# Sample states as the moving operand on four column groups, state increments on four row groups, in a fused hybrid decoder step

## What is computed

```python
def step(S, inp):                       # one chunk; the sample has one chunk of 4 tokens
    qg_c, kd_c, u_c, w_c, qk_c, gl_c = inp
    v_new = u_c - w_c @ S
    o = qg_c @ S + qk_c @ v_new
    S = S * gl_c + kd_c.T @ v_new
    return S, o
```

## Time and profile before

| | |
|---|---|
| median of 3 runs | 1909.12 us (1908.06 to 1911.35) |
| the profiled execution | 1911.12 us |
| its span, first to last instruction | 1909.3 us |
| mean granted TensorE clock | 0.995 |
| TensorE busy (PE) | 1800.0 us, 94% |
| VectorE busy (DVE) | 556.5 us, 29% |
| ScalarE busy (ACT) | 388.0 us, 20% |
| HBM read | 519.14 MB |

### The profile page before, as it was taken

One profiled execution on the slowest core, in us unless ns is written; L12 is line 12 of the kernel. 1 busy time (PEld: TensorE's weight loads), 2 busy tenths in 40 slices (PEclk: granted clock), 3 DMA queues, 4 the chain that ended last, 5 costly groups with the idle time before them and its releaser, 6 DMA issues.

```text
span 1909.3 us, 22816 instructions
## 1 busy us (share of the span) xinstructions
PE 1800.0 (94%) x8060; PEld 933.9 (49%) x8060; DVE 556.5 (29%) x1811; ACT 388.0 (20%) x922; POOL 19.5 (1%) x37
## 2 busy tenths in 40 slices
PE   7999999999998999999999999999999999999998
PEld 4777777777775433433333333333333333334333
DVE  2334434434434200321323213232132311224113
ACT  1424524524523111311000111001010010002103
POOL 0000000000000000000000000000000000000000
PEclk9999999999999999999999999999999999999999
DMA  8333433433404461599999999999999999999401
GB/s 253 100 95 102 126 94 103 124 94 104 124 28 149 152 250 73 199 419 428 427 428 427 427 427 427 427 427 427 428 426 427 425 427 425 424 424 384 168 22 50
DMA packets 208462, 519.92 MB, mean 272 GB/s; under 512 B 18664, under 2 KB 139488, under 8 KB 157152
## 3 DMA queue, kind: packets, MB, share of 16 engines
q1 hardware_dynamic: 198160, 513.83, 69.0%
q0 software_dynamic: 2304, 4.86, 0.7%
q10 hardware_dynamic: 7968, 0.83, 0.3%
HBM read 519.14 MB, written 12.26 MB: 278 GB/s over the span
## 4 chain that ended last, share of the span: by engine, by line
PE 79%; DMA 17%; DVE 2%; ACT 1%; issue 1%; SPq 0%; DVEq 0%; ACTq 0%
PE ps L582 75%; DMA ring<-in_w_down_dram 17%; PE ps L585 3%; DMA x<-in_x_sample_dram 0%; PE ps L1082 0%; ACT hb L1210 0%; ACT ring L1210 0%; SPq L477 0%; DMA pp_rows<-hb 0%; DVE ring L1694 0%; PE ps L710 0%; PE ps L730 0%; DVE ring L1745 0%; PE ps L731 0%; DVE x L2011 0%
## 5 line engine op out<-in xcount | busy, mean ns | idle before, releaser
L582 PE MATMUL ps<-ring,hT 128*64 128x512 f32 x2048 | 457.0, 596 | 25.6 <-DMA ring<-in_w_up_dram 25.6
L582 PE MATMUL ps<-hT,ring 128*128 128x288 f32 x1536 | 410.1, 414 | 0.0
L582 PE MATMUL ps<-ring,mixT 128*64 128x512 f32 (+2 forms) x1408 | 365.6, 598 | 35.9 <-DMA ring<-in_w_down_dram 25.6
L582 PEld LDWEIGHTS ps<-hT,ring 128*128 128x128 f32 x1536 | 283.3, 192 | 70.4 <-issue 0.5
L582 PEld LDWEIGHTS ps<-ring,hT 128*64 128x64 f32 x2048 | 145.7, 137 | 308.4 <-issue 305.8
L582 PEld LDWEIGHTS ps<-ring,mixT 128*64 128x64 f32 (+2 forms) x1408 | 124.8, 144 | 240.2 <-issue 238.3
L582 PE MATMUL ps<-ring,hb 128*128 128x512 f32 (+2 forms) x512 | 143.7, 512 | 0.0
L582 PE MATMUL ps<-mixT,wpT 128*128 128x512 f32 (+1 forms) x384 | 130.1, 601 | 0.0
L582 PEld LDWEIGHTS ps<-ring 128*128 128x128 f32 (+3 forms) x880 | 115.7, 186 | 29.0 <-DVE ring L1767 7.9
L582 PE MATMUL ps<-ring 128*128 128x128 f32 (+3 forms) x880 | 123.8, 272 | 1.7 <-DVE ring L1754 1.6
L1210 ACT ACTIVATE ring<-ps 128x256 f32<-128x256 f32 (+5 forms) x176 | 47.5, 310 | 294.4 <-PE ps L582 256.8
(11 more groups left out here) (248 smaller groups left out, 1096.7 us busy)
## 6 DMA issues: line engine op xcount, KB each, us to landing
ring<-in_w_gate_dram SPq DMA_DIRECT2D x128, 1024.0 KB, 22.5
ring<-in_w_up_dram SPq DMA_DIRECT2D x128, 1024.0 KB, 24.4
ring<-in_w_down_dram SPq DMA_DIRECT2D x128, 1024.0 KB, 22.0
ring<-in_w_in_dram SPq DMA_DIRECT2D x48, 1024.0 KB, 5.6
ring<-in_w_out_dram SPq DMA_DIRECT2D x16, 1024.0 KB, 11.0
ring<-in_w_ple_gate_dram SPq DMA_DIRECT2D x16, 1024.0 KB, 13.3
hb<-in_state_delta_dram SPq DMA_DIRECT2D x8, 512.0 KB, 5.2
out_dram<-hb SPq DMA_DIRECT2D x8, 512.0 KB, 3.7
```

Of the source, the lines that this page charges most:

```text
L582: return pe.matmul(out, lhsT, rhs, start=start, stop=stop)
```

## The change

For the sample, the roles in the products with the states are swapped and the small matmuls are placed on parts of the array:

- Step 3: the state becomes the moving operand (128 columns), the 32-column block of WQ the weights, each sequence on column group b % 4 of the array. The two halves (b < 4, b >= 4) accumulate in one bank; WQ is zero except for each sequence's own 8 columns. ScalarE copies the result out as SQs (`SQ_r`).
- Step 4: v is corrected by tokens: the matmul of XTs4 (four copies of XTs side by side) and vb, plus a matmul of a constant selecting matrix `pick_w` and SQs in the same bank. The transpose and VectorE's subtraction go. The result has the 32 tokens four times, on all 128 partitions.
- Step 5: the q.S part is added by one more matmul with `pick_q`. VectorE's addition and `os_r` go.
- Step 6: Vm is two masked copies on 128 partitions; four matmuls of 32 rows on 256 columns, each on its own row group and with its own bank (3 to 6). They wait for `os_p` too; the sum of squares goes to bank 7 and waits for `S2_r` too.
- The triangular solve's first level (L1763 to L1767) writes XTs in four copies, four operations of VectorE where there was one, before the one that lets TensorE go on (`lev_new`).
- Step 1 makes the sample's k on all four partition groups (4 matmuls for one transpose), step 2 loses the uT matmul, and the prologue's sample decays are made four times.

```diff
@@ constants
-              ("seq", row // SEQ_LEN == np.arange(SEQS)[None, :]),
+              ("seq", row % SAMPLE // SEQ_LEN == 2 * (row // SAMPLE) + np.arange(2)[None, :]),
+              ("pick_w", -1.0 * (row == solved_row(col % SAMPLE))), ("pick_q", (row == solved_row(col) + SEQ_LEN)[:, :SAMPLE]),
@@ tensor: prologue
-            mm(ps[0:SAMPLE, 3, 16:24], C("btriu", SAMPLE), g[0:SAMPLE, 2, :])
-            mm(ps[0:SAMPLE, 3, 40:48], C("ball", SAMPLE), g[0:SAMPLE, 2, :]).then_inc(dec["prep_mm"], 1)
+            for r in range(0, P, 32):
+                mm(ps[r:r + 32, 3, 16:24], C("btriu", SAMPLE), g[0:SAMPLE, 2, :])
+                last = mm(ps[r:r + 32, 3, 40:48], C("ball", SAMPLE), g[0:SAMPLE, 2, :])
+            last.then_inc(dec["prep_mm"], 1)
@@ tensor: head, step 1
-                    pe.transpose(ps[0:n, 5, t * P:(t + 1) * P], qk[:, 1, off:off + n], C("ident"))
+                    if t < 2:
+                        pe.transpose(ps[0:n, 5, t * P:(t + 1) * P], qk[:, 1, off:off + n], C("ident"))
+                    else:
+                        for r in range(0, P, 32):
+                            mm(ps[r:r + 32, 5, t * P:(t + 1) * P], qk[:, 1, PROMPT:TOK], C("ident"))
@@ step 2
-                mm(ps[:, 5, PROMPT:TOK], vb[0:SAMPLE, 2, :], XTs[0:SAMPLE, :])
@@ step 3
-                    last = mm(ps[:, 2, b * 8:(b + 1) * 8], Sold[:, b, :], WQ[:, b, :])
+                    g = 32 * (b % 4)
+                    last = mm(ps[g:g + 32, 2, 0:P], WQ[:, 32 * b:32 * b + 32], Sold[:, b, :], b < 4, b >= 4)
@@ step 4
-                pe.wait_ge(E["vnT_r"], h1)
-                pe.transpose(ps[0:SAMPLE, 5, 0:P], vnTs, C("ident")).then_inc(E["vnTT"], 1)
+                pe.wait_ge(E["SQ_r"], h1)
+                mm(ps[:, 5, 0:P], XTs4[0:SAMPLE, :, :], vb[0:SAMPLE, 2, :], True, False)
+                mm(ps[:, 5, 0:P], C("pick_w"), SQs, False, True).then_inc(E["vns_mm"], 1)
@@ step 5
-                mm(ps[:, 4, PROMPT:TOK], vns[0:SAMPLE, :], QKTs[0:SAMPLE, :]).then_inc(E["o_mm"], 1)
+                mm(ps[:, 4, PROMPT:TOK], vns[0:SAMPLE, :], QKTs[0:SAMPLE, :], True, False)
+                mm(ps[:, 4, PROMPT:TOK], SQs, C("pick_q"), False, True).then_inc(E["o_mm"], 1)
@@ step 6
-                for q in range(2):
-                    last = mm(ps[:, 5 + q, :], kd[0:SAMPLE, 2, :], Vm[0:SAMPLE, 4 * q:4 * q + 4, :])
+                pe.wait_ge(E["os_p"], h1)
+                for r in range(4):
+                    rows = slice(32 * r, 32 * r + 32)
+                    last = mm(ps[:, 3 + r, 0:2 * P], kd[rows, 2, :], Vm[rows, 0:2, :])
                 last.then_inc(E["dS_mm"], 1)
                 pe.wait_ge(E["osq_r"], h1)
-                mm(ps[:, 3, 0:TOK], C("ones"), osq).then_inc(E["oss_mm"], 1)
+                pe.wait_ge(E["S2_r"], h1)
+                mm(ps[:, 7, 0:TOK], C("ones"), osq).then_inc(E["oss_mm"], 1)
@@ scalar: head
-                f(uTs, ps[:, 5, PROMPT:TOK])
...
+                act.wait_ge(E["SQ_mm"], h1)
+                f(SQs, ps[:, 2, 0:P]).then_inc(E["SQ_r"], 1)
                 pieces_out()
-                act.wait_ge(E["vnTT"], h1)
-                f(vns[0:SAMPLE, :], ps[0:SAMPLE, 5, 0:P]).then_inc(E["vns_r"], 1)
+                act.wait_ge(E["vns_mm"], h1)
+                f(vns, ps[:, 5, 0:P]).then_inc(E["vns_r"], 1)
...
-                act.wait_ge(E["os_r"], h1)
+                act.wait_ge(E["os_p"], h1)
                 f(osq, oS, ACT.Square).then_inc(E["osq_r"], 1)
@@ vector: head, level 1
-                        tt(XTs[0:SAMPLE, :], XTs[0:SAMPLE, :], ps[0:SAMPLE, 7, 256:256 + SAMPLE], ALU.subtract)
+                        for r in range(3, -1, -1):
+                            tt(XTs4[0:SAMPLE, r, :], XTs[0:SAMPLE, :], ps[0:SAMPLE, 7, 256:256 + SAMPLE], ALU.subtract)
@@ vector: head, steps 3 to 6
-                v.wait_ge(E["SQ_mm"], h1)
-                SQ = ps[:, 2, 0:64].rearrange("p (b c) -> p b c", c=8)
-                sq4 = lambda a: a.rearrange("p (b c) -> p b c", c=SEQ_LEN)
-                tt(sq4(vnTs), sq4(uTs), SQ[:, :, 0:SEQ_LEN], ALU.subtract).then_inc(E["vnT_r"], 1)
...
-                for b in range(SEQS):
-                    last = ts(Vm[0:SAMPLE, b, :], vns[0:SAMPLE, :], C("seq", SAMPLE)[:, b:b + 1], None, ALU.mult)
+                for i in range(2):
+                    last = ts(Vm[:, i, :], vns, C("seq")[:, i:i + 1], None, ALU.mult)
                 last.then_inc(E["Vm_r"], 1)
-                v.wait_ge(E["os_p"], h1)
-                os4 = sq4(oS[:, PROMPT:TOK])
-                tt(os4, os4, SQ[:, :, SEQ_LEN:], ALU.add).then_inc(E["os_r"], 1)
+                v.wait_ge(E["o_mm"], h1)
                 v.wait_ge(E["s2_st"], snap(h * 16 + 1))
...
-                              in1=ps[:, 5 + b // 4, (b % 4) * P:(b % 4 + 1) * P], op0=ALU.mult, op1=ALU.add)
+                              in1=ps[:, 3 + b // 2, (b % 2) * P:(b % 2 + 1) * P], op0=ALU.mult, op1=ALU.add)
```

More of the change, by code:

```diff
@@ L57, in _constants, with solved_row @@
     same = (row // SEQ_LEN) == (col // SEQ_LEN)
+    def solved_row(token):
+        b = token // SEQ_LEN
+        return 32 * (b % 4) + 2 * SEQ_LEN * (b // 4) + token % SEQ_LEN
     parts = [("ident", row == col), ("triu", row <= col), ("before", row < col), ("ones", row >= 0 * col),
@@ L214, in trunk @@
         Xs = w(SAMPLE)
-        XTs = w(SAMPLE)
+        XTs4 = w(4, SAMPLE)
+        XTs = XTs4[:, 0, :]
         T1 = w(2, P)
@@ L219, in trunk @@
         wT = w(2, P)
-        uTs = w(SAMPLE)
-        WQ = w(SEQS, 2 * SEQ_LEN)
+        WQ = w(272)
+        WQ_cols = WQ.rearrange("p (h x) -> p h x", h=2)[:, :, 0:P].rearrange("p h (g c) -> p h g c", g=4)
+        SQs = w(P)
         S1 = w(P)
@@ L224, in trunk @@
         vn1 = w(P)
-        vnTs = w(SAMPLE)
         vns = w(P)
-        Vm = w(SEQS, P)
+        Vm = w(3, P)
         Sold = w(SEQS, P)
@@ L317, in trunk @@
                  "ln_sq", "vn_r", "mixA_mm", "mixA_r", "uw_mm", "uw_cp", "WQ_r", "S1_mm", "S1_r", "SQ_mm", "wS_mm",
-                 "vn1_r", "vnT_r", "vnTT", "Vm_r", "vns_r", "o_mm", "S2_r", "Sn_r", "os_p", "os_r", "osq_r", "oss_mm", "rn_r", "or_r",
+                 "vn1_r", "SQ_r", "vns_mm", "Vm_r", "vns_r", "o_mm", "S2_r", "Sn_r", "os_p", "osq_r", "oss_mm", "rn_r", "or_r",
                  "mixB_r")
@@ L901, in between @@
                         last.then_inc(R["lgT_mm"], 1)
-            pe.wait_ge(E["os_r"], HEADS)
+            pe.wait_ge(E["os_p"], HEADS)
             for k in range(KT - 1):
@@ L1328, in head @@
                     f(kbg[0:n, t, :], kt, scale=hs[0:n, t, 3:4])
-                    f(kd[0:n, t, :], kt, scale=hs[0:n, t, 4:5])
+                    f(kd[:, t, :], ps[:, 5, t * P:(t + 1) * P], scale=hs[:, t, 4:5])
                     last = f(vb[0:n, t, :], vt, scale=hs[0:n, t, 2:3])
@@ L1350, in head @@
                 f(us[:, :, :], ps[:, 5, 0:256].rearrange("p (t n) -> p t n", t=2))
-                f(uTs, ps[:, 5, PROMPT:TOK])
-                f(WQ[:, :, 0:SEQ_LEN], ps[:, 6, PROMPT:TOK].rearrange("p (b c) -> p b c", c=SEQ_LEN))
+                f(WQ_cols[:, :, :, 0:SEQ_LEN], ps[:, 6, PROMPT:TOK].rearrange("p (h g c) -> p h g c", h=2, c=SEQ_LEN))
                 f(wT[:, 1, :], ps[:, 6, P:2 * P]).then_inc(E["uw_cp"], 1)
@@ L1367, in head @@
                 act.wait_ge(E["oss_mm"], h1)
-                rstd([(orn, ps[:, 3, 0:TOK], P)], P, E["or_r"])
+                rstd([(orn, ps[:, 7, 0:TOK], P)], P, E["or_r"])
                 pieces_out()
@@ L1607, in _ @@
             v.memset(pre[:, :, :, :], 0.0).then_inc(M["wpt_T"], 1)
+            v.memset(WQ, 0.0)
             ch(v.memset(raw[:, :, 0:PAD], 0.0))
@@ L1648, in _ @@
             cp(pre[:, 5, 0:2, :], ps[:, 3, 0:16].rearrange("p (t c) -> p t c", t=2))
-            cp(pre[0:SAMPLE, 5, 2, :], ps[0:SAMPLE, 3, 16:24])
+            cp(pre[:, 5, 2, :], ps[:, 3, 16:24])
             cp(pre[:, 6, 0:2, :], ps[:, 3, 24:40].rearrange("p (t c) -> p t c", t=2))
-            ch(cp(pre[0:SAMPLE, 6, 2, :], ps[0:SAMPLE, 3, 40:48]))
+            ch(cp(pre[:, 6, 2, :], ps[:, 3, 40:48]))
             ch.wait()
             tt(pre[:, 7, 0:2], pre[:, 6, 0:2], pre[:, 5, 0:2], ALU.subtract)
-            v.memset(pre[:, 7, 2], 0.0)
             ch(v.memset(zero[:, :], 0.0))
             ch.wait()
-            tt(pre[0:SAMPLE, 7, 2], pre[0:SAMPLE, 6, 2], pre[0:SAMPLE, 5, 2], ALU.subtract).then_inc(dec["prep_v"], 1)
+            tt(pre[:, 7, 2], pre[:, 6, 2], pre[:, 5, 2], ALU.subtract).then_inc(dec["prep_v"], 1)
             v.wait_ge(dec["prep_a"], 3)
@@ L1794, in head @@
                         tt(mixT[:, bass.ds(h, 1), :].rearrange("p a n -> p (a n)"), mA, uT, ALU.mult).then_inc(E["mixA_r"], 1)
-                cp(WQ[:, :, SEQ_LEN:], qg[:, PROMPT:TOK].rearrange("p (b c) -> p b c", c=SEQ_LEN)).then_inc(E["WQ_r"], 1)
-                v.wait_ge(E["SQ_mm"], h1)
-                SQ = ps[:, 2, 0:64].rearrange("p (b c) -> p b c", c=8)
-                sq4 = lambda a: a.rearrange("p (b c) -> p b c", c=SEQ_LEN)
```

(3 more changed lines are left out.)

## The result

| | before | after |
|---|---|---|
| median of 5 runs | 1909.12 us (1908.06 to 1911.35) | 1900.06 us (1898.35 to 1902.88) |
| the profiled execution | 1911.12 us | 1899.4 us |
| its span | 1909.3 us | 1897.6 us |
| the fourth head, from start to start | 71.69 us | 70.78 us |
| TensorE busy | 1800.0 us, 94% | 1790.4 us, 94% |

The ratio of after to before is 0.9954 (0.9942 to 0.9966). The forecast was 1900.2. A second pair of runs gave 1910.46 before and 1900.47 after, ratio 0.9947 (0.9933 to 0.996).

What follows compares the result with a forecast made beforehand. Heads bound by TensorE's own stream, experts by their transfers: -1.14 us a head, -9.1 in 8 heads, prologue about +0.2, sum -8.9, so 1909.1 to 1900.2 us; range 1898 to 1903, 8 in 10 1896.0 to 1905.0.

Steps and rivals of the forecast that it cites:

- a loss of 0.2: Prologue: 12 more passes from its four-fold small matmuls were to add about 0.2 us outside the heads.
- the added waits: TensorE's waits on `SQ_r`, `os_p`, `S2_r` and Vm: projection passes were to cover them, so priced at nothing.
- visit: TensorE's switch to part of the array and back: 0.10 us per shape change, about 0.22 in all among short passes.
- Rivals A: Increments on row groups: weights load in turn, 0.90 us a head; sum -5.1, median 1904.0 us; chance 0.12.
- B: Increments: row groups run in turn, 1.72 us a head as before; sum +1.4, median 1910.5 us; chance 0.07.
- C: Increments: row groups in turn, each load in the open, 2.5 us; sum +7.7, median 1916.8 us; chance 0.05.
- Rival D: Short column-group passes run in turn at 0.06 us each; sum -2.8, median 1906.3 us; chance 0.04.
- The solve's delay: Solve's first level: four VectorE copies instead of one make `lev_new` 0.29 us later, uncovered on TensorE; +0.29 a head.
- The experts: Stretch bound by its DMA transfers: moves forward with shorter heads, as long as before, neither eating nor adding gain.
- the clock's spells: Last head: the clock falls while TensorE waits; a spell more or less is worth up to 2 us.
- the 0.56: Increments on row groups, by the skill's 3.07 times: 0.56 us a head, making the sum -7.9.

Runs made afterwards that it cites:

- e6: Changed kernel with the XTs4 and vb matmul issued earlier, beside the other 32-row matmul, and `pick_w` adding to it there; 1894.8 us, ratio 0.9924.
- e1: Changed kernel with all four increment matmuls on rows 0 to 31, one row group in turn (wrong results); 1909.91 us, ratio 1.0002 to before.
- e2: Changed kernel with all eight state matmuls on column group 0, in turn (wrong results); 1909.77 us, ratio 1.0001 to before.
- e3: Changed kernel with XTs written once in the solve's first level and its other three copies made behind the second level; 1898.88 us, ratio 0.9942.
- e9: The kernel before, run and profiled again without an edit; 1909.74 us, ratio 1.0001 to its other runs.
- e7: Changed kernel with VectorE writing the sample's k four times and one 128-column transpose replacing four matmuls; 1896.0 us, ratio 0.9928.
- e10: The changed kernel, run and profiled again without an edit; 1900.47 us, ratio 0.9947 to before.

## Why the prediction was right, and where its sum was off

The median moved by 9.06 us, where the sum said 8.9. That it came out so close is luck. Two errors stand against each other: the heads gained 7.3 us (8 x 0.91) and not 9.1, and about 1.8 us came from outside their sum, where I had a loss of 0.2. A head of 70.78 us is also outside the 0.15 either way that I had allowed for 70.55. The mechanism was right: both kinds of groups run side by side, and the added waits are covered.

| step of the sum, us a head | predicted | measured |
|---|---|---|
| step 1, sample's k on four groups | +0.33 | +0.35 |
| solve, copies ahead of `lev_new` | +0.29 | +0.29 |
| step 2, uT gone | -0.22 | -0.22 |
| step 3, states on column groups | -1.03 | -1.02 |
| step 4, tokens and `pick_w` | +0.56 | +0.72 |
| step 5, `pick_q` | +0.22 | +0.24 |
| step 6, increments on row groups | -1.29 | -1.27 |
| the head | -1.14 | -0.91 |

- **Step 4 is the term that was mis-sized,** +0.72 for +0.56. I priced its visit as one "among short passes", 0.22. That price comes from 32-row matmuls with 32 moving columns: in before's records of them the first pass after the change of shape is followed by the next in 0.133 us (302.759 to 302.892). In step 4 the moving operand has 128 columns, and in after's records the first pass takes 0.214 to the next start, once on the way in (341.11 to 341.33) and once more on the way back (341.53 to 341.74), beside 0.20 for 0.11 at each change itself. Twice 0.10 above the 0.11 of a pass, where I had twice 0.02: 2 x 0.08. I read the 0.10 as the pass's load in the open, since loads follow each other in 0.108 us there (PEld, 341.112 and 341.220); no run separates the load from the rest of the change. e6 shows the price from the other side, where the same two passes cost 0.22 once they stand with others of their shape.
- The other terms are each off by 0.02 or less. The 0.23 that the head misses is thus 0.16 of step 4 and 0.07 of the rest.
- **Row groups run side by side:** e1 against after, 1.92 for 0.64. In after's records the four passes of a round start at 347.249, .256, .262 and .269, the second round 0.30 behind the last of them. Without the first pass's surplus (0.10) and the change of shape (0.10) the 0.64 is 0.44 us of streaming, for the 0.43 that I took. Rivals A (0.90), B (1.72) and C (2.5) all fall.
- **Column groups too:** e2 against after, 1.86 for 0.57. Rival D asked for 0.06 a short pass in turn; a round of four takes 0.11.
- **The solve's delay** is that of the three extra copies: the load waits 0.51 for 0.22, and 0.22 again in e3. I had expected to see PE idle for 0.3 us there, and it is idle for 0.06: the busy time of a projection pass reaches 0.16 us behind the next start (0.41 for 0.245) and covers 0.16 of the delay in the profile, and the last 0.07 shows behind the first pass (314.68 to 315.23 in after, 0.48 in e3). The head is longer by the whole 0.29 all the same.
- **The added waits** cost nothing. No wait on `SQ_r`, `os_p`, `S2_r` or `Vm_r` stands in the timeline; the head's time without a matmul rose by 0.06 us, and that is the solve's. The end of a head keeps its 4.24 us.
- **The experts** neither ate nor added: their stretch starts earlier and is at 1.01 of the DMA engines, as before. That it is 1.3 us shorter in after goes with the spell at its start in before: half the clock from 803.34 to 805.0 is 0.8 us of it (an estimate), and the rest is open. It is as short in e1 (944.28), whose heads are slower than before's and whose trace has no spell there.
- **Outside the sum** the clock's spells moved. I had allowed 2 us for them in the range, unsigned. I had also read the fall in before's last head as one within a wait; it comes at 586.5, 0.3 us behind the wait's end, and TensorE works through the spell. In the profiled executions they came out in favour of after in the last head (1.6 us), the routing and the experts (1.2 to 1.7 and 1.3), and against it at the end (1.6). e1 says the same: its heads should cost 3.0 us over before (8 x 0.38), its median equals before's, and its trace has no spell in the routing, the experts or the last stretch. e2's median equals before's too, but its trace has them in the routing and in the last stretch, so the account doesn't close for every run. Why the clock falls at one wait and not at another these runs do not settle. So a gain of some 2 us in this kernel can't be read from its median; the head's window shows 0.1 us.

The Trainium skill, "TensorE: Matmul & The Clock Gate", section Measured speedup vs the span model, states 3.07 times for four row tiles on 512 columns. e1 and after give 1.92 / 0.64 = 3.0 on 256 columns, with the costs of the shape in both. Without them it is 1.72 / 0.44 = 3.9. So the trace agrees with that figure only when the shape's costs are in it; the 0.56 that the prediction worked out for step 6 by it, with the change of shape priced apart, was 0.44 here.

## What to carry to other kernels

Price small matmuls on parts of the array by rounds of four, and then add every change of tile shape on its own: 0.10 us to change, and the surplus of the first pass. In these traces (float32) that is 0.10 us for a pass with 128 columns of weights and 128 or more moving ones, and 0.02 where the moving columns are 32 (step 1) or the weights have 32 columns (step 3: the second round starts 0.133 behind the first, the next ones 0.109). Put matmuls of one shape side by side before packing them, and put extra copies behind the signal that the array waits for. When a change has two ideas in it, run each alone: here one earned all of the gain and the other, as it stood, none. With its two costs mended (e3 and e6) the swap would be worth 0.67 us a head, an estimate from 0.29 + 0.38; no run has it without the increments.

## What the runs showed of the hardware that I had not expected

- Four passes on four row groups, each into its own bank and on all 128 partitions of it, start 5 to 8 ns apart and stream together; so do four on column groups (6 to 7 ns).
- The surplus of a first pass (0.10 us) is paid on the way back to the whole array as well, when the pass has 128 columns of weights and 128 or 288 moving ones: 0.213 to the next start for 0.11, and 0.347 for 0.245 (347.893 to 348.240).
- A transpose whose input has 32 columns changes no shape: 0.11 us in the middle of whole ones (e7), while the 32-column matmuls in its place start 0.20 behind the pass ahead of them, and leave 0.20 for the next.
- From the last head on, spells at half clock (0.50, 1.2 GHz) come with waits of TensorE of 1.6 to 2.9 us; not every such wait brings one. Two executions of one kernel have them at nearly the same places (after and e10) or not quite (before one in the last head, e9 two). One costs 1.6 to 1.7 us where TensorE works through it, and nothing where its next wait absorbs it.
